# The tiles of x packed 256 columns apart, and the constants' buffer moved to the end of the memory

## The reference

```
first model:   h = x
  layer 0: h = h + retention(rmsnorm(h))            q, k: 4 heads of 256; v, gate: 2048 wide
           h = h + sigmoid(rmsnorm(h) @ w_gate0) * (p0 @ w_emb0)
  layer 1: keys and values from rmsnorm(h, kv_norm) @ kv_w; compressed, selected and window branches
           h = h + sparse_attention(rmsnorm(h, nsa_norm) @ nsa_w_in) @ nsa_w_out
           h = h + sigmoid(rmsnorm(h) @ w_gate1) * (p1 @ w_emb1)
  h = rmsnorm(h)
second model:  h = [16 meta tokens; h]              272 rows from here
  u = rmsnorm(h); proj = u @ w_in                   gated delta rule and forgetting attention
  h = h + concat(o_gdn, o_fox) @ w_out
  h = h + (silu(rmsnorm(h) @ w_gate) * (rmsnorm(h) @ w_up)) @ w_down      w_gate, w_up: 1024 x 2816
  return rmsnorm(h)[16:]
```

## Time and profile before

| | us |
|---|---|
| median of 3 runs | 973.38 (972.57 to 976.53) |
| the profiled execution | 973.14 |
| its span, first to last instruction | 971.6 |
| TensorE busy | 956.8 |
| VectorE (DVE) busy | 630.5 |
| ScalarE (ACT) busy | 475.8 |

### The profile page before, as it was taken

How to read it: one execution, slowest core, us unless ns; L and a number is a source line. 1 busy time by engine, 2 the same in 40 slices (tenths; PEclk the granted TensorE clock), 3 DMA queues, 4 the chain that set the end, 5 groups by cost and what they waited for, 6 DMA issues and landing times.

```text
span 971.6 us, 16020 instructions
## 1 busy us (share of the span) xinstructions
PE 956.8 (98%) x6442; PEld 857.4 (88%) x6442; DVE 630.5 (65%) x918; ACT 475.8 (49%) x834; POOL 119.7 (12%) x124
## 2 busy tenths in 40 slices
PE   8999999999999999999999999999999999999997
PEld 8988778878998999998888789989998899999885
DVE  5974457557884655677864477987655666766543
ACT  7335446455545543465554456654434455444432
POOL 1000032010410000101320003312320111111001
PEclk9999999999999999999999999999999999999999
DMA  9735445545556663242015454532011355555551
GB/s 330 281 131 189 158 136 177 183 162 193 179 185 217 252 226 131 94 167 88 1 44 178 169 180 140 173 116 88 1 45 44 130 196 190 202 183 208 178 211 44
DMA packets 23516, 150.55 MB, mean 155 GB/s; under 512 B 3564, under 2 KB 3848, under 8 KB 6168
## 3 DMA queue, kind: packets, MB, share of 16 engines
q1 hardware_dynamic: 23104, 149.39, 44.2%
q10 hardware_dynamic: 344, 0.18, 0.1%
HBM read 148.50 MB, written 1.05 MB: 154 GB/s over the span
## 4 chain that ended last, share of the span: by engine, by line
PE 89%; DVE 6%; ACT 3%; issue 1%; DMA 1%; POOL 0%; SPq 0%; ACTq 0%; POOLq 0%; DVEq 0%
PE psum L723 85%; DVE ring_parts L1984 2%; PE psum L802 1%; DVE R L2286 1%; ACT R L1736 1%; DVE PTb_parts L2257 1%; DMA h<-in_x 1%; PE psum L1444 0%; PE psum L1129 0%; ACT xT_parts L1759 0%; DVE small L2202 0%; ACT high_parts L1559 0%; ACT R L1566 0%; ACT R_parts L1742 0%; DVE R L2296 0%
## 5 line engine op out<-in xcount | busy, mean ns | idle before, releaser
L1984 DVE TENSOR_TENSOR ring_parts<-ring,high_parts 128x1024 fp32r<-128x1024 f32 (+1 forms) x272 | 333.6, 1265 | 157.3 <-ACT high_parts L1559 156.2
L1559 ACT CAST high_parts<-ring 128x1024 fp32r<-128x1024 f32 x268 | 268.2, 1051 | 197.3 <-PE psum L723 160.6
L723 PE MATMUL psum<-xT_parts,high_parts 128*128 128x256 f32 (+1 forms) x1024 | 230.0, 286 | 2.3 <-DVE ring_parts L1984 1.9
L723 PE MATMUL psum<-xT_parts,ring_parts 128*128 128x256 f32 (+1 forms) x704 | 201.8, 287 | 0.0
L723 PE MATMUL psum<-high_parts,R_parts 128*128 128x512 f32 (+1 forms) x592 | 176.9, 373 | 0.0
L723 PEld LDWEIGHTS psum<-xT_parts,high_parts 128*128 128x128 f32 x1024 | 173.6, 190 | 3.7 <-DVE ring_parts L1984 2.3
L723 PE MATMUL psum<-R_parts,high_parts 128*128 128x256 f32 x832 | 156.5, 277 | 0.0
L723 PE MATMUL psum<-high_parts,xT_parts 128*128 128x512 f32 x480 | 155.5, 399 | 0.0
L723 PEld LDWEIGHTS psum<-xT_parts,ring_parts 128*128 128x128 f32 x704 | 133.2, 189 | 0.1
L723 PEld LDWEIGHTS psum<-R_parts,high_parts 128*128 128x128 f32 x832 | 130.6, 188 | 0.0
L723 PEld LDWEIGHTS psum<-high_parts,R_parts 128*128 128x128 f32 (+1 forms) x592 | 104.9, 179 | 20.7
(11 more groups left out here) (330 smaller groups left out, 1125.1 us busy)
## 6 DMA issues: line engine op xcount, KB each, us to landing
ring<-in_weights SPq DMA_DIRECT2D x135, 1024.0 KB, 4.9
h<-in_x SPq DMA_DIRECT2D x4, 256.0 KB, 4.4
ring<-in_weights SPq DMA_DIRECT2D x4, 256.0 KB, 5.6
ring<-in_weights SPq DMA_DIRECT2D x2, 512.0 KB, 7.1
G<-in_gains SPq DMA_DIRECT2D x2, 512.0 KB, 7.5
out<-xn SPq DMA_DIRECT2D x2, 512.0 KB, 2.6
R<-in_ret_tabs SPq DMA_DIRECT2D x1, 768.0 KB, 13.7
tab<-in_tabs SPq DMA_DIRECT2D x1, 663.5 KB, 6.0
```

Of the source, the lines that this page charges most:

```text
L723: return pe.matmul(out, lhsT, rhs, start=first, stop=last, skip_group_check=True)
L1559: act.copy(as_r(hi), value).then_inc(sem("units_high"), 1)
L1984: return dve.tensor_tensor(as_r(value), value, value_of(hi), ALU.subtract)
```

## The change

It does three things.
- Up to the end of the sparse attention the tiles of x lie 256 columns apart in `xT` and `xT2` (`into_x`, `into_kv`, `into_nsa`, `turned_p`, and the reads through the new `tokens_src`). The 16 meta columns of each tile are kept apart, 128 columns behind the eight tiles (`meta_kept`).
- From the second embedding gate on (`ple(1, ...)`, `into_attn`) the tiles are 272 columns apart as before. One copy on ACT for `xT` and one on DVE for `xT2` puts the meta columns in front of their tiles (`meta_moved`) before the first tile is written there.
- `tab` is declared behind `small`, so all buffers from `par` to `small` start 5824 bytes earlier.

In the built program after the change `xT` starts at 95616, `xT2` at 104320, `R` at 113024 and `PTb` at 178560. All four are 128 modulo 256, like `ring` and `high`, and so are all tiles of x up to the end of the sparse attention.

```diff
-        tab = sb("tab", NTAB)
         par = sb("par", NPARAM)
...
         small = sb("small", 568)
+        tab = sb("tab", NTAB)
...
         def into_x(kt):
+            return kt_cols(xT, kt, 0, T, T), kt_cols(xT2, kt, 0, T, T)
+
+        def into_attn(kt):
             return kt_cols(xT, kt, M, T), kt_cols(xT2, kt, M, T)
 
+        def meta_kept(buf, kt):
+            return kt_cols(buf, kt, 0, M, M, KD * T)
+
+        def meta_moved(buf):
+            return as_r(buf[:, :].rearrange("p (k w) -> p k w", k=KD)[:, :, 0:M]), value_of(
+                buf[:, KD * T:KD * TM].rearrange("p (k w) -> p k w", k=KD))
+
         def into_kv(kt):
-            return kt_cols(xT, kt, M, T), R[:, R4 + kt * T:R4 + (kt + 1) * T]
+            return kt_cols(xT, kt, 0, T, T), R[:, R4 + kt * T:R4 + (kt + 1) * T]
 
         def into_nsa(kt):
-            return kt_cols(xT2, kt, M, T), PTb[:, 2048 + kt * T:2048 + (kt + 1) * T]
+            return kt_cols(xT2, kt, 0, T, T), PTb[:, 2048 + kt * T:2048 + (kt + 1) * T]
...
+            def tokens_src(k, c0, n):
+                tile_ready("x", k)
+                return kt_cols(xT, k, c0, n, T), kt_cols(xT2, k, c0, n, T)
...
-                project_a([("rqk", n)], x_src, M, T)
+                project_a([("rqk", n)], tokens_src, 0, T)
...
-                    project_b([("rg", c, t) for t in range(TT)], x_src, rows, KD)
+                    project_b([("rg", c, t) for t in range(TT)], tokens_src, rows0, KD)
...
+                    if n == 1 and c == 0:
+                        wait(aux, ("xT_ple1", 0))
+                        act.copy(*meta_moved(xT)).then_inc(sem("meta_high"), 1)
+                        act.wait_ge(sem("meta_high"), 1)
                     high_parts(f"xT_ple{n}", slice(2 * c, 2 * c + 2))
...
                 if n == 1:
                     dve.wait_ge(sem("gain1_in"), 16)
+                    wait(aux, ("xT_ple1", 0))
+                    own.then_wait(dve.tensor_copy(*meta_moved(xT2)))
                 low_parts(f"xT_ple{n}")
```

More of the change, by code:

```diff
@@ L485, in turned_p @@
             n = i % 2 * 4 + br * 2
-            return (xT[:, n * TM:(n + 2) * TM].rearrange("p (f t) -> p f t", f=2)[:, :, M:TM],
+            return (xT[:, n * T:(n + 2) * T].rearrange("p (f t) -> p f t", f=2),
                     PTb[:, n * T:(n + 2) * T].rearrange("p (f t) -> p f t", f=2))
@@ L525, in two_models_kernel @@
         turned("xT_kv", range(4), (into_kv, gain_of("kv_norm")), (into_nsa, gain_of("nsa_norm")))
-        turned("xT_ple1", range(4), (into_x, gain_of("ple_norm1")))
-        turned("xT_attn", range(4), (into_x, lambda kt: attn_gain[:, kt:kt + 1]))
+        turned("xT_ple1", range(4), (into_attn, gain_of("ple_norm1")))
+        turned("xT_attn", range(4), (into_attn, lambda kt: attn_gain[:, kt:kt + 1]))
         turned("xT_ffn", range(4), (into_ffn, gain_of("ffn_norm_w_2")))
@@ L897, in _ @@
                         ins = parts3(product, bank[:, half * T:(half + 1) * T], w(k, slice(half * P, (half + 1) * P)),
-                                     x_src(k, M, T), half == 0 and k == 0, k == KD - 1)
+                                     tokens_src(k, 0, T), half == 0 and k == 0, k == KD - 1)
             main.full(ins, ("rqk", 0))
             for n in range(1, 8):
-                project_a([("rqk", n)], x_src, M, T)
+                project_a([("rqk", n)], tokens_src, 0, T)
                 if n == 1:
@@ L909, in _ @@
             aux.full(ins, "meta")
-            project_b([("rv", 0, t) for t in range(TT)], x_src, rows, KD)
+            project_b([("rv", 0, t) for t in range(TT)], tokens_src, rows0, KD)
             def qk_tile(which, hd, half, c0, n):
@@ L924, in _ @@
             for c in range(1, 4):
-                project_b([("rv", c, t) for t in range(TT)], x_src, rows, KD)
+                project_b([("rv", c, t) for t in range(TT)], tokens_src, rows0, KD)
             def retention_values(hd):
@@ L997, in ple @@
                 need("x", f"xT_ple{n}", 4)
-                project_b([("pg", n, 0, t) for t in range(TT)], x_src, rows, KD)
-                project_b([("pg", n, 1, t) for t in range(TT)], x_src, rows, KD, ready)
+                src, rows_ = (x_src, rows) if n else (tokens_src, rows0)
+                project_b([("pg", n, 0, t) for t in range(TT)], src, rows_, KD)
+                project_b([("pg", n, 1, t) for t in range(TT)], src, rows_, KD, ready)
             def turn_kv(c):
@@ L2061, in _ @@
             for kt in range(KD):
-                ins = dve.tensor_scalar(as_r(kt_cols(xT, kt, 0, M)), bank[:, kt * M:(kt + 1) * M],
+                ins = dve.tensor_scalar(as_r(meta_kept(xT, kt)), bank[:, kt * M:(kt + 1) * M],
                                         param("attn_norm_w_2", kt), None, ALU.mult)
@@ L2065, in _ @@
             for kt in range(KD):
-                ins = dve.scalar_tensor_tensor(as_r(kt_cols(xT2, kt, 0, M)), bank[:, kt * M:(kt + 1) * M],
-                                               param("attn_norm_w_2", kt), value_of(kt_cols(xT, kt, 0, M)), ALU.mult,
+                ins = dve.scalar_tensor_tensor(as_r(meta_kept(xT2, kt)), bank[:, kt * M:(kt + 1) * M],
+                                               param("attn_norm_w_2", kt), value_of(meta_kept(xT, kt)), ALU.mult,
                                                ALU.subtract)
```

## The result

The changed kernel takes 979.04 us, the median of 7 runs (977.34 to 982.02), where the kernel before takes 973.38 us beside it (7 runs, 972.02 to 976.53). The ratio is 1.0049, 95% interval 1.0032 to 1.0065. The forecast was 965.3 us and a gain. The range held the time, but the sign was wrong, and the time is close to that of the rival "the new base is a bad one" (979.8 us).

The account below looks back on a forecast made before the run. TensorE, busy 98% of the span, was taken as the bound, through the pace of its instructions. From 973.1 us, -6.3 (`project_a`), -1.5 (`project_b` over x) and 0 (base) gave 965.3 us, range 959 to 980.

Parts of the forecast that it names:

- the new base is a bad one: Rival: both streams at 128 modulo 256 run only slowly, costing feed-forward and `project_b` over R; +6.7, 979.8 us; chance 0.18.
- The reading of the profile: TensorE's matmuls: a steady address relation of the two read streams allows a fast rhythm, 340 instead of 351 to 355 ns.
- the address isn't the reason: Rival: stages differ in pace for another cause, such as engines or transfers beside them; nothing changes, 973 us; chance 0.12.
- the base: Buffers behind `side_sb` start 5824 bytes earlier, x, R and PTb move from 64 to 128 modulo 256; taken as 0.
- The tiles 256 columns apart: Steady x tiles up to the end of the sparse attention: `project_a` -6.3 us, `project_b` with x as weights -1.5 us.
- the split rival: Streams split between fast and slow rhythm, in half of `project_a`'s x triples or the feed-forward; 969 us; chance 0.23.
- The better-base rival: Rival: the new base is better than any seen, 7 ns less per triple for 512 + 352 triples; 959.3 us; chance 0.05.
- The meta copies: One new copy each on ACT and DVE at the second embedding gate; nothing if covered, 1.2 us without that cover.
- Nothing was late next: Stages with x never leave TensorE waiting; DVE and ACT, busy 65% and 49%, would not become late.

Follow-up runs that it names:

- the constants back in front: The changed kernel with the constants' buffer `tab` declared in front of the large buffers again, x tiles still 256 columns apart; 970.63 us, ratio 0.996 to the kernel before.
- the two kernels with the weights at 192: The constants-back kernel with everything 64 bytes further (967.62 us), and one with xT, xT2 at 64 and R, PTb at 192 modulo 256 (984.81 us).

## Why the prediction was wrong

**The reading of the profile was right.** TensorE's pace depends on the addresses. With the constants back in front, most of the x stages took the 340 ns and 687 ns of the earlier trace rows. That, and the two kernels with the weights at 192, answers the rival "the address isn't the reason", and what the rule in the Trainium skill ("SBUF — State Buffer", section "Who interferes with whom") would have made of it: an independent read port for each stream and no waiting on anyone, so no change. The runs show one relation that port independence doesn't cover, the distance of the two streams modulo 256 bytes: equal instructions take 340 to 360 ns a triple, and 680 to 703. Against the sum of that rule, no change, stands +0.5%, clear of the interval. Why the distance matters is not settled. No run shows what inside the memory or the engine goes by it.

**The failed step is the base.** The prediction put the move from 64 to 128 at zero, "since both steady relations seen show the shorter pace". Two samples of eight were extended to a third, and the kind of each was not kept apart. The 340 ns came from x moving at distance -64, the 686.8 ns from x as weights at the same distance -64. "A moving tile at 64 over weights at 128 and the reverse" sounded like two relations and was one. At distance 0 a moving x runs at 360.0 ns. That is outside the upper bound I took from the earlier trace rows, 352.9 ns: the cost in the feed-forward was bounded at 4.5 us and is 6.8. And it reached the 512 triples of x as well: +0.7 and +2.6 us in place of -1.9 and -4.3. Nor is being steady what makes the pace short: all steady distances but -64 run at 350 to 360 ns (save two half-units at +64), and the stepping tiles lie between.

**The bad-base rival was near in time and half right.** Its 6.7 us were 4.5 + 1.9 + 0.3 (feed-forward, over R, x moving) and nothing over x. Measured are 6.8, -1.3, +3.3 and -2.7, so 6.1 us. The signs over R and over x are the opposite: where the matrix moves, distance 0 is the best place of all, 680.0 ns. The errors cancel.

**The tiles 256 columns apart.** The terms for their own part, at the old base: -6.3 and -1.5 us, measured with the constants back -4.9 and -1.6. About 1.0 of the missing 1.4 us are units in the longer rhythm, which the split rival named. The rest is in three query units whose triples stand between other matmuls, so that the pace of x gives little there. It had its price from the feed-forward network, where in fact nothing changed, and it had not seen that `project_b` has two rhythms as well: 686.7 and 700.0 ns, +0.8 us at the attention's output.

**The better-base rival** took its 7 ns from nine starts in 1.00 us, but eight of these are transposes of 128 columns, and a triple has 256 each. No kernel shows a triple with moving x under 340.0 ns.

**The meta copies** were put at nothing, bounded by 603 ns each, and took 300 and 220 ns under the plain matmuls, with no wait. Right.

**Nothing was late next.** DVE and ACT had room, and TensorE's wait for low parts stayed at 1.9 us. Right.

## What to carry to other kernels

When TensorE is hardly ever idle, measure its pace from the starts of equal instructions, stage by stage, and set it beside where the moving tile and the weights lie to each other, modulo 256 bytes: here that is worth 6% where x moves and 3% where the matrix does. A buffer moved for any other reason shifts all behind it, so an edit of the layout is two edits, and each must be priced by itself for each kind of use. Don't price an unseen relation by seen ones; run a map of it, with a few unused columns between the buffers.

## What was not expected of the hardware

- The pace goes by the distance of the two streams modulo 256 in steps as fine as 32 bytes, and the order isn't monotone. The best distance for a moving x (-64, 340.0 ns) is not the best for x as weights (0, 680.0 ns).
- At distance -64 the same instructions have two stable rhythms, 340.0 and 353.3 ns (686.7 and 700.0 with 512 columns). All four are multiples of 20/3 ns. A short matmul ahead is enough to switch, and run to run variation at the start too. Other distances have a second rhythm as well: +64 (353.3 and 340), -96 (356.0 and 352.0), and 128 over x (697.1 and 700.7).
- The granted clock drops to half (1.2 GHz) for a few microseconds, nearly always in the second model (near 650, between 660 and 675, near 745 us, and at the very end), and which of these drops occur differs from run to run, in kernels with and without the change. The same program (constants back) has, apart from the end, one of 6.8 us in one profile and three of 3.4 us in the other. A drop of 3.4 us costs about 1.5 us. The runs of the kernel before spread over 7.6 us (971.68 us at a mean clock of 0.999, 979.3 us at 0.992), more than the difference to be measured. By an estimate from these drops (0.007 of 972 us is four of them) about 6 of the 7.6 us are the clock.
